# A two-layer GLA, MLA and GQA trunk: the condition after the first squares, the GQA maxima from 128 rows, w_out rounded in two parts

## What is computed

```python
shift, scale, gate = jnp.split(jax.nn.silu(c) @ w_mod[l] + b_mod[l], 3, axis=-1)
h = rms_norm(x, norm_w[l]) * (1.0 + scale[:, None, :]) + shift[:, None, :]
u = split_cols(h @ w_in[l], IN_COLS)
...   # the same for the context tokens, with c_ctx
y_a = gla_branch(...)        # gated linear attention, 4 heads, chunks of 64
y_b = mla_branch(...)        # 6 heads, keys of 64 + 32 (rotary) columns
y_c = gqa_branch(...)        # 6 query heads of 64 columns on 2 key heads
x = x + gate[:, None, :] * (jnp.concatenate([y_a, y_b, y_c], axis=-1) @ w_out[l])
```

## Time and profile before

| | us |
|---|---|
| median of 3 runs | 1052.6 (1052.39 to 1053.06) |
| profiled execution | 1052.06 |
| its span (first to last instruction) | 1050.1 |
| PE busy | 963.9 |
| DVE busy | 510.0 |
| ACT busy | 421.4 |
| POOL busy | 136.5 |
| mean granted PE clock | 0.971 of full |

### The profile page before, as it was taken

One profiled execution on the slowest core, in us unless ns is written; L12 is line 12 of the kernel. 1 busy time (PEld: TensorE's weight loads), 2 busy tenths in 40 slices (PEclk: granted clock), 3 DMA queues, 4 the chain that ended last, 5 costly groups with the idle time before them and its releaser, 6 DMA issues.

```text
span 1050.1 us, 12554 instructions
## 1 busy us (share of the span) xinstructions
PE 963.9 (92%) x4563; PEld 668.7 (64%) x4563; DVE 510.0 (49%) x872; ACT 421.4 (40%) x753; POOL 136.5 (13%) x158
## 2 busy tenths in 40 slices
PE   2789999999899999899899889899997999999896
PEld 2468889888465455455478677689774545445475
DVE  2535534532864444556452563543548444555443
ACT  4424433322113554656831432533321244555902
POOL 3000000001250001000640200000013300100720
PEclk9899999999889999999999899899999899999998
DMA  9802220311300232022053211130513000022022
GB/s 331 282 16 65 62 75 6 101 41 47 114 1 1 94 130 97 1 81 81 1 172 73 81 30 51 43 98 1 137 40 126 1 0 1 1 81 80 1 100 81
DMA packets 67867, 74.12 MB, mean 71 GB/s; under 512 B 6148, under 2 KB 47456, under 8 KB 67680
## 3 DMA queue, kind: packets, MB, share of 16 engines
q1 hardware_dynamic: 61392, 60.17, 18.2%
q0 software_dynamic: 4016, 12.77, 3.4%
q10 hardware_dynamic: 2400, 0.38, 0.2%
HBM read 69.11 MB, written 4.19 MB: 70 GB/s over the span
## 4 chain that ended last, share of the span: by engine, by line
PE 81%; DVE 7%; ACT 4%; issue 3%; DMA 2%; POOL 1%; ACTq 1%; DVEq 0%; POOLq 0%
PE pv L1692 10%; PE bank L1483 9%; PE bank L1484 9%; PE bank L1485 8%; PE bank L1743 6%; PE bank L1653 3%; PE bank L1774 3%; PE bank L1776 3%; PE bank L1775 3%; PE bank L1620 2%; PE bank L1600 2%; DMA W<-in_w_in 2%; PE bank L1669 2%; PE bank L1521 2%; PE bank L1523 2%
## 5 line engine op out<-in xcount | busy, mean ns | idle before, releaser
L1483 PE MATMUL bank<-hA_parts,W_parts 128*128 128x512 f32 (+1 forms) x496 | 181.7, 366 | 11.7 <-DVE h_low_parts L1016 9.1
L1484 PE MATMUL bank<-hA_parts,W_parts 128*128 128x512 f32 (+1 forms) x496 | 175.2, 353 | 0.0
L894 ACT ACTIVATE hA<-bank 128x512 f32<-128x512 f32 (+1 forms) x168 | 92.5, 561 | 82.1 <-PE bank L1743 56.1
L1290 DVE TENSOR_REDUCE mxp<-bank 128x1 f32<-128x384 f32 x192 | 96.4, 550 | 47.4 <-PE bank L1653 47.1
L1483 PEld LDWEIGHTS bank<-hA_parts,W_parts 128*128 128x128 f32 x496 | 95.7, 193 | 30.8 <-issue 14.0
L1485 PE MATMUL bank<-h_low_parts,W_parts 128*128 128x512 f32 (+1 forms) x310 | 109.9, 354 | 0.0
L1484 PEld LDWEIGHTS bank<-hA_parts,W_parts 128*128 128x128 f32 x496 | 95.6, 193 | 13.7 <-issue 2.2
L1692 PE MATMUL pv<-hA,vg 128*128 128x512 f32 (+1 forms) x168 | 83.1, 576 | 6.8 <-ACT hA L894 6.4
L1692 PE MATMUL pv<-hA,XA 128*128 128x512 f32 (+1 forms) x168 | 81.0, 563 | 2.4 <-ACT hA L894 2.3
L1023 DVE TENSOR_TENSOR W_parts<-W,W_parts 128x1024 fp32r<-128x1024 f32 x44 | 53.5, 1221 | 32.9 <-ACT W_parts L631 32.8
L1308 DVE SCALAR_TENSOR_TENSOR hA<-pv,hA 64x512 f32<-64x512 f32 (+1 forms) x36 | 21.6, 599 | 90.8 <-ACT hA L837 90.6
(11 more groups left out here) (254 smaller groups left out, 1836.6 us busy)
## 6 DMA issues: line engine op xcount, KB each, us to landing
W<-in_w_in SPq DMA_DIRECT2D x39, 512.0 KB, 4.0
W<-in_w_mod SPq DMA_DIRECT2D x8, 2048.0 KB, 8.0
W<-in_w_out SPq DMA_DIRECT2D x4, 2048.0 KB, 7.8
gqk<-in_w_mod SPq DMA_DIRECT2D x2, 1536.0 KB, 10.5
cqkv<-in_w_mod SPq DMA_DIRECT2D x2, 1536.0 KB, 14.7
XA<-in_x SPq DMA_DIRECT2D x4, 512.0 KB, 7.7
XA<-in_x POOLq DMA_DIRECT2D x4, 512.0 KB, 6.6
x_between_layers<-XA POOLq DMA_DIRECT2D x4, 512.0 KB, 2.9
```

Source lines behind the costliest of these rows:

```text
L894: act.activation(prob[slot % 4][:, 0:nq], ps("sc", l, h, q0, kt)[:, 0:nq], ACT.Exp, scale=MLA_SCALE if h < MLA_H else GQA_SCALE)\
L1290: dve.tensor_reduce(mxp[:, t, half:half + 1], ps("mx", l, h, q0, t, half)[:, 0:384], AX, ALU.max).then_inc(*up("part_max", l, h, q0, t, half))
L1483: pe.matmul(p[:, 0:c[1]], high[:, k, :], h_hi[:, k, toks], start=(k == 0), stop=False)
L1484: pe.matmul(p[:, 0:c[1]], low[:, k, :], h_hi[:, k, toks], start=False, stop=False)
```

## The change

Four things.

- ACT issues the identity's DMA first; the tanh and its table set are gone. The condition's silu is made after the sixth square, from the functions of the loaded set: Abs, Exp and Ln give log-sigmoid, a second Exp the sigmoid, DVE multiplies. PE transposes the small vectors after the fifth token tile.
- On PE, modulation block 3 goes after slice k = 1 and its turn after k = 2.
- The maxima of a GQA head are taken from `q_both` (128 rows) instead of the first 96 rows of `q_high`; ACT fills `q_both` in part 0 and `q_high` in part 2. `k_low` moves into `h_low`, and POOL writes its pads earlier.
- Block 0 of w_out is rounded one piece per unit at eight named places in heads 8 to 10 (`W_HIGH_AT`; the number beside the head is the latent unit), block 1 after the last `y_high`. The rounded pieces lie in other buffers.

```diff
+W_HIGH_AT = [(8, 5), (9, 1), (9, 2), (9, 3), (9, 4), (10, 1), (10, 2), (10, 3)]
...
-        k_twice, k_low = ([e[:].rearrange("p f h c -> p (f h c)")[:, o * T:(o + 1) * T]
-                           for e in (wuq_parts, wukv_parts)] for o in range(2))
+        k_twice = [e[:].rearrange("p f h c -> p (f h c)")[:, 0:T] for e in (wuq_parts, wukv_parts)]
+        k_low = [h_low[:, 1 + g, :] for g in range(2)]
...
@@ gpsimd: behind head_ones(2), no longer behind round_k(l, 5)
+                for g in range(2):
+                    if g:
+                        pool.wait_ge(*at("k_pad", l, 0, 1))
+                    pool.memset(k_low[g][64:96, :].bitcast(F32), 0.0).then_inc(*up("k_pad", l, g, 0))
+                    pool.memset(k_low[g][96:97, :].bitcast(F32), 1.0).then_inc(*up("k_pad", l, g, 1))
+                pool.wait_ge(*at("k_pad", l, 1, 1))
...
@@ scalar
-            act.wait_ge(*at("vec_turned"))
-            act.activation(ct[:, 0, :], vt[:, 0:16], ACT.Tanh, scale=0.5).then_inc(*up("cond_tanh"))
-
             act.preload_act_table_set("natural_log_exp_and_others")
...
+                    act.wait_ge(*at("vec_turned"))
+                    act.activation(ct[:, 0, :], vt[:, 0:16], ACT.Abs).then_inc(*up("cond_abs"))
+                    act.wait_ge(*at("cond_abs"))
+                    act.activation(ct[:, 0, :], ct[:, 0, :], ACT.Exp, scale=-1.0).then_inc(*up("cond_exp"))
+                    act.wait_ge(*at("cond_exp"))
+                    act.activation(ct[:, 0, :], ct[:, 0, :], ACT.Ln, bias=ones[:, 0:1]).then_inc(*up("cond_ln"))
+                    act.wait_ge(*at("cond_logsig"))
+                    act.activation(ct[:, 1, :], ct[:, 1, :], ACT.Exp).then_inc(*up("cond_sig"))
                     turned_copy(TILES - 1)
...
+                        act.activation(q_both[b][0:64, lat], src, ACT.Copy).then_inc(*up("q_both", l, h))
+                    if part == 2:
                         act.activation(q_high[b][0:64, lat], src, ACT.Copy).then_inc(*up("q_high", l, h))
-                    if part == 2:
-                        act.activation(q_both[b][0:64, lat], src, ACT.Copy).then_inc(*up("q_both", l, h))
...
-                        c = j - 3 if h == heads[-2] else j + len(todo) - 4 if h == heads[-1] and j else -1
-                        if 0 <= c < KD:
-                            w_high(2 * c // KD, (2 * c % KD, 2 * c % KD + 1))
+                        u = j - len(todo) + TILES
+                        if h in (8, 9, 10) and (h, u) in W_HIGH_AT:
+                            w_high(0, (W_HIGH_AT.index((h, u)),))
...
                 y_high((6, 7))
+                w_high(1, range(KD))
...
@@ tensor
-                if k in (0, 2):
-                    mod(0, 2 + k // 2)
-                if k in (1, 3):
-                    mod_turn(0, 2 + k // 2)
+                if k == 0:
+                    mod(0, 2)
+                if k == 1:
+                    mod_turn(0, 2)
+                    mod(0, 3)
+                if k == 2:
+                    mod_turn(0, 3)
...
-                            pe.wait_ge(*at("q_high", l, h))
+                            pe.wait_ge(*at("q_both", l, h))
+                            pe.wait_ge(*at("q_low", l, h))
                             pe.wait_ge(*at("k_once", l, (h - MLA_H) // 3))
                             pe.wait_ge(*at("k_twice", l, (h - MLA_H) // 3))
-                            pe.wait_ge(*at("q_pad", l, h % 2))
-                            q, k = q_high[h % 2][0:96, :], k_twice[(h - MLA_H) // 3][0:96, :]
+                            q, k = q_both[h % 2], k_twice[(h - MLA_H) // 3]
```

More of the change, by code:

```diff
@@ L313, in pieces @@
             return [e[:, c:c + 512] for e in tensors for c in range(0, e.shape[1], 512)]
-        w_hi = [pieces(gqk_parts[:].rearrange("p f t -> p (f t)"), glav_parts[:].rearrange("p t c -> p (t c)")),
-                pieces(rounded[:].rearrange("p f t -> p (f t)"), glaqk_parts[:].rearrange("p f t -> p (f t)"),
-                       sq_parts[:].rearrange("p a b -> p (a b)"))]
+        w_hi = [pieces(glav_parts[:].rearrange("p t c -> p (t c)"), glaqk_parts[:].rearrange("p f t -> p (f t)"),
+                       sq_parts[:].rearrange("p a b -> p (a b)")),
+                pieces(gqk_parts[:].rearrange("p f t -> p (f t)"), rounded[:].rearrange("p f t -> p (f t)"))]
         heads = list(range(MLA_H + GQA_H))
@@ L506, in _ @@
                     round_k(l, h)
[L508 to L515, removed]
                 for b in range(2):
@@ L551, in _ @@
         def _(act):
+            act.dma_start(con[:, C_ID:C_ID + P], a["consts"][:, C_ID:C_ID + P]).then_inc(*dma("ident_in"))
             def rows(r, n, src):
@@ L564, in _ @@
                     act.dma_start(vec[r:r + 2, half * 64:half * 64 + 64], a[name]).then_inc(*dma("vec_in"))
-            act.dma_start(con[:, C_ID:C_ID + P], a["consts"][:, C_ID:C_ID + P]).then_inc(*dma("ident_in"))
             src = a["w_in"][0].rearrange("(k p) n -> p k n", p=P)
@@ L846, in w_high @@
                         if n == 0:
-                            act.wait_ge(*at("q_both", l, heads[-1]))
+                            act.wait_ge(*at("filled", "o", l, TILES - 1))
+                            act.wait_ge(*at("y_gla", l, TILES - 1))
+                        else:
+                            act.wait_ge(*at("q_high", l, heads[-1]))
                             act.wait_ge(*at("k_low", l, 1))
                             act.wait_ge(*at("q_low", l, heads[-1]))
[L851 to L855, removed]
                         act.activation(w_hi[n][k], W[:, i % 2, k, :], ACT.Copy).then_inc(*up("w_hi", l, n, k))
@@ L939, in _, with condition @@
         def _(dve):
[L940 to L952, removed]
+            def condition():
+                dve.wait_ge(*at("filled", "vec"))
+                dve.tensor_copy(vt[:], ps("vec")[:, 0:V_ROWS]).then_inc(*up("vec_turned"))
+                let_go(("vec",), "vec_turned")
+                dve.wait_ge(*at("vec_turned"))
+                dve.tensor_scalar(vth[:], vt[:], 0.5, None, ALU.mult).then_inc(*up("vec_half"))
+                dve.wait_ge(*at("cond_ln"))
+                dve.scalar_tensor_tensor(out=ct[:, 1, :], in0=vt[:, 0:16], scalar=0.0, in1=ct[:, 0, :],
+                                         op0=ALU.min, op1=ALU.subtract).then_inc(*up("cond_logsig"))
+                dve.wait_ge(*at("cond_sig"))
+                dve.wait_ge(*at("pool_init", "end"))
+                dve.tensor_tensor(sc[:, :, 0:2].rearrange("p k s -> p s k"),
+                                  vt[:, 0:16].rearrange("p (s k) -> p s k", s=2),
+                                  ct[:, 1, :].rearrange("p (s k) -> p s k", s=2), ALU.mult)\
+                    .then_inc(*up("cond_silu"))
             def mod_cols(l, b):
@@ L1007, in _ @@
                     turned_copy(t - 1)
+            condition()
             turned_copy(TILES - 1)
@@ L1421, in block_wait @@
                 pe.wait_ge(*at(f"w_half{i % 2}", i))
[L1423 to L1426, removed]
             def mod(l, b):
@@ L1465, in mod_turn @@
                         close(pe.matmul(q[:], sel[:, s, :], modrow, start=True, stop=True), "gate", l, b - 4, s)
+            pe.wait_ge(*at("ident_in"))
             for t in range(TILES):
@@ L1474, in _ @@
                     close(mm, "xr", t, half)
+                if t == TILES - 2:
+                    pe.wait_ge(*at("vec_in"))
+                    p = open_("vec")
+                    close(pe.transpose(p[:, 0:V_ROWS], vec, ident[0:V_ROWS, 0:V_ROWS]), "vec")
             def unit_products(p, l, item, c, ks):
@@ L1735, in _ @@
                             if h >= MLA_H:
-                                pe.wait_ge(*at("q_both", l, h))
-                                pe.wait_ge(*at("q_low", l, h))
+                                pe.wait_ge(*at("q_high", l, h))
                                 pe.wait_ge(*at("k_low", l, (h - MLA_H) // 3))
                                 pe.wait_ge(*at("k_pad", l, 1, 1))
+                                pe.wait_ge(*at("q_pad", l, h % 2))
                         p = open_("sc", l, h, q0, kt)
```

## The result

The changed kernel took 1069.84 us (median of 4, 1069.15 to 1071.03) against 1052.49 for the kernel before on the same chip: ratio 1.0166, 95% interval 1.0149 to 1.0184. It is slower, as forecast, but by 17.4 us where the prediction had 8, and it lies above the range of 1051 to 1066. The profiled execution took 1071.03, with a span of 1069.2 against 1050.1: 19.1 us to find.

A forecast was written before the change was run, and what follows sets the result against it. TensorE, holding 81% of the chain, was taken as the bound, so whatever makes it wait costs in full. Gains of -13.1 and losses of +21.0 gave +7.9 on 1052.06, so 1060.0, median 1060.5; range 1051 to 1066.

The forecast's parts named there:

- Maxima from 128 rows: GQA heads: TensorE waits for the low part of q before the maxima; 19.3 us lost, 1.1 gained in layer 0's head 10.
- The rival in which the wait isn't felt: GQA heads: VectorE sets the end of a head, so late maxima cost nothing; near 1039.5 us, chance 0.12.
- Sum: -3.2 - 1.7 - 1.1 - 1.7 - 5.4 = -13.1: All gains: start idle, start half clock, layer 0's head 10, layer 0's attention end, layer 1's attention end.
- layer 0's end: Head 11 of layer 0: without w_out pieces on ScalarE the outputs start sooner; gain 1.7 us.
- Layer 1's -5.4: End of layer 1's attention: values end 1.7 us sooner, low parts of Y keep up for 3.7; bounds 3 and 6.
- block 1, the memsets and the reload of X: Late w_out subtractions, GpSimd's earlier k_low memsets and the later X reload all cost 0, being covered.
- the tail did not fill up: Output tail rival: late subtractions and X reload make TensorE wait for a bank; 3 to 7 us more, chance 0.08.
- Layer 1's two longest stands: Layer 1, heads 5 and 6: stands of 3.4 and 4.1 us cause one clock fall, 1.7 us; bounds 0 and 3.4.
- The clock falls more often, or stays low after the start: TensorE's clock rival: 1.7 to 3.4 us more, 1062 to 1064 us, chance 0.15.
- With that gap gone I also take back the half-clock stretch: Start, after the 3.70 us idle: the 3.3 us at half rate from 65.0 us go; gain 1.7 us.
- the small unit still lands near 29: Start, sign of being right: the small w_in unit's DMA keeps its landing time, 29.35 us before; gain 0.
- The small unit lands sooner: Start rival: the w_in unit's landing follows ScalarE's work; up to 5.9 us more gain, about 1055, chance 0.10.

The follow-up runs named there:

- experiment 3: Changed kernel with VectorE's subtraction for the next head's q_low put ahead of the last head's normalise: 1037.89 us, ratio 0.9854; once more 1039.87, ratio 0.9864.
- experiment 4: Kernel before with only the maxima part of the change (128 rows, the wait for q_low, q_both copied ahead of q_high): 1086.63 us, ratio 1.0337.
- experiment 5: Changed kernel with its maxima part alone undone (96 rows of q_high, q_low waited for by the scores): 1040.82 us, ratio 0.9883.
- the first trace: The changed kernel's first profiled execution, nothing further edited: 1071.03 us, span 1069.2.
- all three traces with open stalls and 128 rows: Changed kernel (1069.84 us), the same again (1070.11), and the kernel before with only the maxima part (1086.63).
- experiment 2: Changed kernel with grouped maxima from the 64 rounded rows alone, their wait for q_low kept: 1109.82 us, ratio 1.0543.
- the second: The changed kernel traced again, unedited, on another chip's runs: 1070.11 us, ratio 1.0183.
- the warm start: Kernel with q_low subtracted ahead of the normalise, plus 14 and 16 idle TensorE products in the start: 1036.07 us, ratio 0.9851.

## Why the prediction was right or wrong

Right: that the kernel is slower, and by which wait. The step "Maxima from 128 rows" gave 19.3 us for eleven low parts and -1.1 for head 10 of layer 0, 18.2 net; the table has 18.7 (188.6 - 169.9). It holds head by head: with half of the half-clock time taken off, heads 5 to 10 grew by 1.7, 1.8, 1.7, 1.5, 1.3 and -1.0 us in layer 0 and by 1.6, 2.3, 1.5, 1.5, 2.5 and 2.4 in layer 1, where the walk had 1.8, 1.7, 1.6, 1.4, 1.2, -1.1 and 1.6, 2.8, 1.4, 1.3, 2.3, 2.2. The matmul costs the same from 96 and from 128 rows. The rival in which the wait isn't felt is refuted by experiments 3, 4 and 5.

Right: the gains. "Sum: -3.2 - 1.7 - 1.1 - 1.7 - 5.4 = -13.1" stands against -12.5 of experiment 5, in part by luck: the start gave less than its term and layer 0's end more. Layer 1's -5.4 was met exactly; layer 0's end gave 2.4 for 1.7; block 1, the memsets and the reload of X cost nothing, and the tail did not fill up. The first four low parts of Y, with GpSimd idle, take 0.63 us each instead of 1.50.

Wrong, and it decides: "Layer 1's two longest stands [...] lie around the gap of 3.8 that the clock fell after and above the 2.3 that it did not. I count one fall, 1.7; bounds 0 and 3.4." The term was mis-sized. There were five falls, 8.5 us, in the first trace, and seven, 17, in the next. They came with the stalls of 1.56, 2.21, 1.81 and 1.36 us in layer 0, in all three traces with open stalls and 128 rows; in layer 1 with 3.85 in all three, with 3.26 in two, with 2.38 and 2.28 once each. The step took the length of one gap as what decides, from a fall behind 3.70 us of idle and none behind two shorter ones. It also read those too long: the stretches of 2.3 and 1.8 in the earlier trace rows hold 0.20 and 0.14 us of products, and the idle in them is 2.10 and 1.67. The rival "The clock falls more often, or stays low after the start", at 0.15 and 1.7 to 3.4 us, was the right mechanism, priced too low. In the one trace with the stalls filled no fall is left, which shows that TensorE's idle is the cause.

Which idle takes the clock down stays open. Length does not sort the cases: in layer 0 the 1.46 of head 9 had no fall in the three traces where the 1.36 of head 10 had one each time, and in the first trace 3.25, 2.38 and 2.29 in layer 1 had none. Other idle close by does not sort them either: head 9 has waits of 0.82 and 0.46 ahead of its stall, head 7, with its fall, has none over 0.3. And the same stall goes both ways: in experiment 2's trace the 1.36 of head 10 stands at full clock.

```profile
539.13 0.58 PE L1663 MATMUL bank<-wukv_parts,hA_parts 64*128 64x256 f32 x2 [1.36 <-issue]
```
```profile
537.70:548.00 10.30, 8.94 (x28) 4.33 (x27) 5.94 (x13) 5.86 (x12) 3.83 (x3) 1.00 0.01 2
```

Wrong in size: the start. -3.2 and -1.7 were forecast, -4.9 in all; the first trace has -2.2, the second -4.1, the start alone -3.4 by its runs. The step that failed is "With that gap gone I also take back the half-clock stretch": the 3.4 us at 65 are gone, but the start has more half clock elsewhere. The idle at 63.7 went as said (0.55 is left, forecast 0.5). "the small unit still lands near 29" failed. So the rival "The small unit lands sooner" had its condition met, but the 2 us did not reach the products: the first one starts at 40.80, before at 40.35, and TensorE ran at half clock from 28.7 to 45.8 where before it did so from 37.6 to 44.4. With the warm start, which fills the idle of 3.3 us in it and cuts that of 4.5 to 2.7, most of that stretch is at full clock.

Not forecast: +1.9 between layer 0's end and layer 1's head 0. The changed kernel has it in all three traces (238.8, 239.2 and 238.8 with the stall filled), the others have 236.8 to 237.4. The same idles of 1.23 and 2.15 us lie there in the changed kernel and in experiment 5, and are followed by 10.2 us at half clock in the one and 3.4 in the other. So it is the clock again; why it differs there stays open. Experiment 2, which has the same parts but 64 rows, doesn't have it.

Against the forecast's +7.9 on the profiled execution: four more falls +6.8, the start +2.7, layer 1's projections +1.9, the wait itself +0.5, layer 0's end -0.7: +11.2, and 7.9 + 11.2 = 19.1.

## What to carry to other kernels

When a product moves to an operand that another engine finishes late, walk the stall through the head, then price the clock too: the stalls of 1.36 to 2.21 us in four of layer 0's heads cost 1.7 to 3.4 more each in three traces of three with 128 rows, and one of them nothing in a fourth with 64. The cure was not to give up the better operand: the late subtraction moved ahead of work that waits anyway, and the wait was gone. And an edit with three parts is worth three runs: here one part's loss, some 29 us (1069.84 - 1040.82, from two chips), hid 12.5 us of gain in the other two.

## What the hardware showed that I had not expected

- Products of 64 rows among products of 128 cost 0.40 us a unit of 1.67, some 16 us in all; with the falls of the clock the kernel with fewer rows was 40 us slower. The kernel before fills its maxima up with 32 rows of zeros, and that pays: without the wait, 96 rows measured 1040.8 and 64 rows 1056.1.
- The stalls of one kernel repeat from execution to execution within 0.02 us, the clock behind them does not: 3.4 or 6.8 us at half clock, or none. So one trace's start or heads can differ by several us from the next one's: the same start took 309.5 to 318.1 us.
- Idle products on TensorE during a wait took every fall out of the heads: 2.1 and 9.0 us less in them than in the two traces of the changed kernel, 6.7 between the medians, though they also delay where the wait is short.
